# A two-block transformer kernel: 64 extra products on TensorE at fifteen places between its stages

## The reference, cut to what matters

```python
for layer in range(DEPTH):                      # first block: layers 0 and 1
    mod = (cond @ ada_w[layer] + ada_b[layer])[:, None, :]
    shift_m, scale_m, gate_m, shift_f, scale_f, gate_f = jnp.split(mod, 6, axis=-1)
    h = rmsnorm(x, norm_mix_g[layer]) * (1.0 + scale_m) + shift_m
    mixed = attention_head_groups(...) if layer % 2 == 0 else gated_deltanet(...)
    x = x + gate_m * mixed
    h = rmsnorm(x, norm_ffn_g[layer]) * (1.0 + scale_f) + shift_f
    x = x + gate_f * swiglu(h, ffn_w_in[layer], ffn_w_out[layer])
x = rmsnorm(x, final_norm_g)
...
for l in range(DEPTH):                          # second block: layers 2 and 3
    hx = modulate(rmsnorm_2(x, norm1_g[l]), sh1, sc1)
    hc = modulate(rmsnorm_2(ctx, norm1_g[l]), csh1, csc1)
    yx, yc = hybrid_mixer(hx, hc, ...)          # window, conv + layernorm, differential, neighbourhood
    x = x + g1 * yx
    x = x + g2 * swiglu_2(modulate(rmsnorm_2(x, norm2_g[l]), sh2, sc2), w_gate[l], w_up[l], w_down[l])
    # the context of 256 tokens takes the same steps in the first of the two
return rmsnorm_2(x, final_g)
```

## Time and profile before

| what | value |
|---|---|
| median of 3 runs | 3706.4 us (3705.87 to 3710.51) |
| span of the profiled execution | 3708.1 us |
| mean granted clock of TensorE | 0.962 |
| busy: PE / DVE / ACT / POOL | 92% / 46% / 31% / 37% of the span |

### The profile page before, as it was taken

The page is one execution under the profiler, slowest core; times in us unless marked ns, Lnnn a source line. Parts: engine busy times, 40 slices in busy tenths (PEclk is TensorE's granted clock), DMA queues, the critical chain, the costliest instruction groups (busy, mean ns, idle before and its releaser), DMA issues. The chain is left out here.

```text
span 3708.1 us, 46261 instructions
## 1 busy us (share of the span) xinstructions
PE 3413.8 (92%) x17788; PEld 2684.9 (72%) x17788; DVE 1708.8 (46%) x3061; ACT 1132.4 (31%) x1422; POOL 1387.8 (37%) x919
## 2 busy tenths in 40 slices
PE   6988999999877779999897998999999998989998
PEld 5864788878667758888695436888899884358887
DVE  5334343437454457474564642744345746521111
ACT  2244322233411132222322343322344322343222
POOL 2323434344553233434231543344410422444434
PEclk9999999999989989999998998999999998999999
DMA  6420344422200014343110001334444320012321
GB/s 227 192 91 9 117 171 152 169 98 91 79 1 1 1 57 170 130 181 142 46 59 33 1 1 57 145 144 171 152 156 173 115 80 1 1 57 84 104 92 62
DMA packets 54653, 353.52 MB, mean 95 GB/s; under 512 B 5856, under 2 KB 6880, under 8 KB 19424
## 3 DMA queue, kind: packets, MB, share of 16 engines
q1 hardware_dynamic: 54208, 349.25, 25.7%
q10 hardware_dynamic: 288, 2.10, 0.1%
HBM read 349.23 MB, written 2.10 MB: 95 GB/s over the span
## 5 line engine op out<-in xcount | busy, mean ns | idle before, releaser
L387 POOL TENSOR_TENSOR W_LO<-ring,W_HI 128x2048 fp32r<-128x2048 f32 (+1 forms) x177 | 729.9, 4124 | 1092.6 <-ACT W_HI L375 1092.6
L443 PE MATMUL PS<-H_HI,W_HI 128*128 128x512 f32 (+1 forms) x1888 | 714.5, 378 | 27.2 <-DVE H_LO L830 21.0
L445 PE MATMUL PS<-H_HI,W_LO 128*128 128x512 f32 (+1 forms) x1888 | 704.7, 373 | 0.0
L444 PE MATMUL PS<-H_LO,W_HI 128*128 128x512 f32 (+1 forms) x1888 | 704.3, 373 | 0.0
L375 ACT ACTIVATE W_HI<-ring 128x2048 fp32r<-128x2048 f32 (+1 forms) x214 | 366.3, 1711 | 481.7 <-PE PS L433 444.7
L443 PEld LDWEIGHTS PS<-H_HI,W_HI 128*128 128x128 f32 x1888 | 360.6, 191 | 91.9 <-issue 32.0
L445 PEld LDWEIGHTS PS<-H_HI,W_LO 128*128 128x128 f32 x1888 | 360.0, 191 | 63.6
L444 PEld LDWEIGHTS PS<-H_LO,W_HI 128*128 128x128 f32 x1888 | 360.6, 191 | 59.7 <-issue 0.2
L872 DVE SCALAR_TENSOR_TENSOR PS<-ring,SC,PS 128x256 f32<-128x256 f32 x768 | 376.3, 490 | 27.0
L431 PE MATMUL PS<-HID_HI,W_HI 128*128 128x512 f32 (+1 forms) x880 | 325.3, 370 | 4.9 <-DVE W_LO L387 4.0
L433 PE MATMUL PS<-HID_HI,W_LO 128*128 128x512 f32 (+1 forms) x880 | 323.7, 368 | 0.0
(11 more groups left out here) (346 smaller groups left out, 5792.7 us busy)
## 6 DMA issues: line engine op xcount, KB each, us to landing
ring<-w_tiles SPq DMA_DIRECT2D x271, 1024.0 KB, 4.8
ring<-d_tiles SPq DMA_DIRECT2D x80, 704.0 KB, 4.1
X<-xT SPq DMA_DIRECT2D x1, 2048.0 KB, 12.3
WORK<-rope_tables ACTq DMA_DIRECT2D x2, 1024.0 KB, 5.7
outT<-H SPq DMA_DIRECT2D x8, 256.0 KB, 2.2
CN<-consts SPq DMA_DIRECT2D x1, 1379.0 KB, 16.3
X<-ctxT SPq DMA_DIRECT2D x1, 1024.0 KB, 9.2
PR<-params SPq DMA_DIRECT2D x1, 465.5 KB, 3.2
```

The costliest lines, as they stand in the source:

```text
L387: eng.tensor_tensor(W_LO[:, b, 0:w], ring[:, g % SLOTS, 0:w], W_HI[:, b, 0:w].bitcast(F32), ALU.subtract).then_inc(sig("tile_split"), 1)
L443: pe.matmul(to, hi[:, cols(k, j)], x_hi(k), start=k == 0, stop=False)
L444: pe.matmul(to, hi[:, cols(k, j)], x_lo(k), start=False, stop=False)
L445: mm = pe.matmul(to, lo[:, cols(k, j)], x_hi(k), start=False, stop=k == n - 1)
```

## The change

A new function issues products of `ones` with the first 512 columns of the constants `CN`, into a bank of PSUM that nobody reads at that point. They signal nothing. They are called behind the fifteen places of the table, 64 products in all.

| place in the program | products | barrier behind it |
|---|---|---|
| end of `pe_out`, behind `pe_norm_sum` (attn_out, gdn_out, out2, out3) | 4 each | no |
| end of `pe_down`, behind `pe_norm_sum` (down001, down101) | 4 each | no |
| end of `pe_block_norm` | 4 | no |
| end of `pe_pairs` (layers 0, 2, 3), after a wait for the heads of the last task but one | 3 each | yes |
| end of `pe_gdn_out` | 3 | yes |
| end of `pe_conv_norm` (layers 2, 3) | 8 each | yes |
| end of `pe_sub_norm` (layers 2, 3) | 4 each | yes |

```diff
+        def pe_hold(pe, o, n):
+            for _ in range(n):
+                pe.matmul(PS[:, o:o + T], ones, CN[:, 0:T], start=True, stop=True)
...
@@ pe_out
             pe_norm_sum(pe, OUT_SUM, sum(w for _, w in segs))
+            pe_hold(pe, 1024, 4)
@@ pe_down
             pe_norm_sum(pe, closing_bank(name), width)
+            if name in ("down001", "down101"):
+                pe_hold(pe, 1024, 4)
@@ pe_pairs
+            pe.wait_ge(sig("pair_heads_done"), b_h + len(tasks) - 1)
+            pe_hold(pe, heads_at(len(tasks)), 3)
@@ pe_gdn_out
                 mm.then_inc(sig("o_turned"), 1)
+            pe_hold(pe, 1024, 3)
@@ pe_conv_norm
             mm.then_inc(sig("y_squares_summed"), 1)
+            pe_hold(pe, 2048, 8)
@@ pe_sub_norm
                 mm.then_inc(sig("heads_summed"), 1)
+            pe_hold(pe, 3072, 4)
```

## The result

| | before | changed |
|---|---|---|
| median | 3709.2 us (8 runs, 3705.9 to 3712.1) | 3718.7 us (8 runs, 3717.9 to 3720.7) |
| ratio | | 1.0028, 95% interval 1.0018 to 1.0038 |
| span of the profiled execution | 3708.1 us | 3716.1 us |
| the same on a second chip | 3703.6 us (21 runs) | 3719.0 us (5 runs), 1.0043, 1.0029 to 1.0056 |

The changed kernel is slower by 9.5 us by the medians, and not level.

A forecast was written before the change was run, and what follows sets the result against it. It took TensorE, 92% busy, as the bound. Losses of 10.8 us less gains of 3.3 gave +7.5 on the traced 3708.1; against the 3706.4 median, +6.1, so 3712.5 us, 0.17% slower, range 3700 to 3719.

The forecast's parts named there:

- up000 / up100 / up200 / up300: Second tiles behind the norms of the four pe_out fall to half clock; losses 1.8, 0, 1.5 (2.9 before halving), 1.5 us.
- pe_gdn_out: Three products ahead of its barrier start at half clock and end after DVE's last operation: +3.3 us, between +1.8 and +4.3.
- pairs of layer 0: Three products end behind DVE at the barrier: +0.4 us, +2.9 at half clock.
- layer 2: pairs, differential norm, out2: Pairs' barrier later by 0.8 us; differential norm gains 1.5 from faster sums; out2's first tile gains 0.6.
- differential norm of layer 3: Already at full clock; its four products end behind DVE at the barrier: +0.9 us.
- biases of layers 2 and 3: Behind the convolution's norm: clock falls again a microsecond into the biases, so -1.0 us each, -2.0 in all.
- The gain, 0: Behind the four pe_out norms, the first tile's 2.6 us saving is hidden, since second tiles wait for W_LO or ACC.
- every half clock was paid for: Rival, 6%: TensorE's end counts at all ten half-clock stretches; 27 us go, less 5 at the barriers: 3684.
- the biases stay at full clock: Rival, 12%: biases behind the convolution's norm gain 6.7 us instead of 1.0 in each of two layers: 3701.
- the clock falls anyway: Rival, 8%: clock falls in the rest of the wait despite the products; no second tile late, barriers remain: 3711.
- Up100 pays it already: 0: Up100's second tile already ran at half clock for 4.9 us before the change, so the change costs nothing there.
- The rival of held barriers at half clock: Rival, 20%: products ahead of barriers run at 1.7 us each and TensorE drains late; about +6, 3718.5.

The follow-up runs named there:

- the second trace of before: The kernel before, unchanged, run and traced again: 0.9995 of the kernel before, span 3698.2 us, 9.9 below its first trace.
- the convolution's: Only the eight products behind the convolution's norm in layers 2 and 3, added to the kernel before: 1.0000.
- the late: Only the products of layers 2 and 3 at the pairs stages (3 each) and differential norms (4 each), added to the kernel before: 1.0003, +1.2 us.
- the layer 0 pairs': Only the three products at the end of layer 0's pairs, added to the kernel before: 1.0004.
- the moved gdn_out products: Three products behind pe_gdn_out's barrier, ahead of the first wait of gdn_out's pe_out, added to the kernel before: 0.9999, -0.3 us.
- all barriers: Only the 20 products ahead of barriers (pairs stages, pe_gdn_out, differential norms), without the convolution's, added to the kernel before: 1.0027, +10.5 us.
- gdn_out's alone: Only the three products at the end of pe_gdn_out, ahead of the barrier, added to the kernel before: 1.0017, +4.7 us.
- the gap was filled: The changed kernel plus more products between first and second tiles of up000, up100, up200 and up300: 1.0023 of the kernel before, 3711.9 us.
- the kernel with early inputs in PSUM and no product: The kernel before with ScalarE rounding the second tile earlier and DVE forming the first ACC earlier, adding in PSUM: 0.9978, 3695.9 us.

## Why the prediction was off

The forecast time of 3712.5 us was 6.2 short of the measured 3718.7: 3.4 of that is the change (forecast +6.1, measured +9.5, and on the second chip +15.4), and 2.8 the level of before. Measured terms are segments of the two traces of the changed kernel, each less those of the second trace of before:

| term | forecast | measured | in the second trace |
|---|---|---|---|
| up000 / up100 / up200 / up300 | 1.8 / 0 / 1.5 / 1.5 | 2.8 / 2.6 / 2.7 / 1.5 | 2.8 / 2.6 / 2.7 / 1.3 |
| pe_gdn_out | 3.3 | 4.2 | 4.5 |
| pairs of layer 0 | 0.4 | 1.7 | 1.7 |
| layer 2: pairs, differential norm, out2 | -1.3 | -2.4 | -2.4 |
| differential norm of layer 3 | 0.9 | 0.9 | 2.1 |
| biases of layers 2 and 3 | -2.0 | -3.2 | -2.3 |
| layers 2 and 3, the rest | 0 | 3.0 | 1.4 |
| layers 0 and 1, the rest | 0 | 4.1 | 3.1 |

- **The gain, 0: right.** The second tiles waited for the same W_LO and ACC, and moving those two together made the kernel faster. The rival that every half clock was paid for is out, and so is the one that the biases stay at full clock: they took 13.05 and 11.54 us (13.90 and 11.63 in the second trace) where that rival needs about 7. That the clock falls anyway is out as well, since the first tiles ran at full clock.
- **"Up100 pays it already: 0": the step that failed.** It took the half clock of one execution for the kernel's. The second trace does not have it, nor do those of the kernels with the convolution's, the late, the layer 0 pairs' or the moved gdn_out products; in two more (all barriers, gdn_out's alone) it fell for 1.6 of the 3.1 us. I had counted up200 as possible luck of the execution and not up100, the one where the luck had fallen the other way. That is 2.6 of the miss. With up200 at its full 2.7, not half, and 1.0 more in up000, the four make 9.6 where I had 4.8.
- **Barriers: a term put at nothing.** TensorE's late drain I priced at 3.3 at gdn_out and 0.4 at layer 0's pairs; it was 2.4 and 0.6. But of layer 0 I wrote that "the following stage waits for O_LO from DVE, so its half clock costs nothing", and of gdn_out's first tile I said nothing at all. In both the half clock now begins later against the work and ends in the part of the first tile that TensorE paces: 1.8 more at gdn_out and 1.1 at layer 0. This step failed too. In layer 2 the gain was 1.1 larger than priced; 0.9 of that lies in the sums behind out2, for which I had no term.
- **The level of before.** The forecast stood on 3706.4 from three runs; eight gave 3709.2 on that chip, 21 to 33 on others 3703 to 3705. The offset of 1.7 between the traced execution and the median was no constant either: two traces of the same kernel lie 9.9 apart. It also set a span against times, and in every execution on record that has both, the time is 1.7 to 1.8 above the span.
- **The rival of held barriers at half clock** gave about the measured time, 3718.5, but by luck and not by its cause: in the late layers the products ran at full clock (2.84 us for the three of layer 2's pairs, 3.60 for the four behind either differential norm). Only gdn_out's began at half.

The last column but one adds up to 17.9 us, the difference of the two spans. Its last row is in part chance of the execution: in the same stages the first trace of before lies 6.1 above the second. Without that row 13.8 are left, inside both chips' intervals (6.7 to 14.1, and 10.7 to 20.7). What stays open is the 3.0 above it. 1.2 are the stretch at the end of layer 2 (last section). Another 1.4 are in the convolution of layer 3, where DVE waits 3.27 us for the transfer of `rope_tables` and not 1.80; no run was made on it. Open too is why the first chip gave 9.5 and the second 15.4, and why places without a product fell when the gap was filled.

## What to carry to other kernels

Before filling an engine's wait to keep its clock, ask what the engine waits for after the work that gets faster: if that input is late, the wait moves there, and so does the fall. Bring the input earlier first; then the filling may not be needed. Ahead of a barrier, filling that ends behind the slowest engine is late for all of them; behind the barrier the same three products cost nothing at gdn_out, the one place tried. And one trace is not the kernel's state at a place that falls by chance.

## What the runs showed of the hardware

- A stretch can fall to half clock far from any change. That of 24.39 us at the end of layer 2, some 590 us behind up200's norm, was at full clock in five traces of kernels with no product behind layer 1 (24.38 to 24.40 us), and took 25.6 to 25.8 us in four of the seven with some; two others paid 1.5 just ahead of it. The products are not the only thing that does this: the kernel with early inputs in PSUM and no product took 24.8 there. Why is open. Before, and the changed kernel:

```profile
2900.82:2925.21 24.39, 20.48 (x103) 16.74 (x103) 15.44 (x26) 12.47 (x20) 11.00 (x6) 1.00 0.25 87
```
```profile
2906.28:2931.86 25.58, 23.09 (x103) 18.77 (x103) 14.90 (x26) 12.48 (x20) 11.00 (x6) 0.87 0.23 80
```

- DVE's additions with both tensors in SBUF stood still beside GpSimd (9.30 us for six); with one of them in PSUM they did not (3.12). The six in each kernel (nanoseconds, least/median/most):

```profile
L889 DVE SCALAR_TENSOR_TENSOR HIDDEN<-ring,SC,HIDDEN x6: 484/940/4873, 1358.6 to 1367.4; 128x256 f32<-128x256 f32 x6
```
```profile
L891 DVE SCALAR_TENSOR_TENSOR PS<-ring,SC,PS x6: 490/490/490, 1352.9 to 1355.5; 128x256 f32<-128x256 f32 x6
```

The Trainium skill states it ("SBUF — State Buffer", section "SBUF: two separate sides"): an operation of VectorE with two inputs in SBUF and one of GpSimd that reads SBUF lock each other out for a whole instruction. The trace agrees: one addition took 4.87 us where others take 0.48, beside a W_LO of GpSimd that took 4.62, as long as beside the additions in PSUM. The kernel before sums ACC with one input in PSUM (L872), so its traces show nothing of this.
